# Three input projections by seven half-size products, with compression's input first, and a rearranged routing stretch

## The reference, cut to what matters

```python
proj = rmsnorm(x, g_mix) @ w_in                      # 256 tokens x 1024, w_in 1024 x 4896
q, k_cmp, v_cmp, k_slc, v_slc, k_win, v_win, g_nsa, x_m, o_pre, i_pre, f_pre, gate_a, gate_b = split(proj)
y_a = nsa_mixer(...)       # compress k_cmp/v_cmp (two small layers, gelu), softmax over 15 blocks,
                           # plus 8 heads over all 256 keys
y_b = mlstm_mixer(...)     # conv over x_m, silu, per head recurrence in parallel form, sigmoid(o_pre)
x = x + (sigmoid(gate_a) * (y_a @ w_up_a) + sigmoid(gate_b) * (y_b @ w_up_b)) @ w_o_mix
x = x + cross_attention(rmsnorm(x, g_x), rmsnorm(mem, g_mem))
logits = rmsnorm(x, g_ffn) @ w_router + b_router     # 32 experts, top 4, ties by index
y = sum over the 4 chosen experts of gate * down(swiglu(x @ w_gu[e] + b_gu[e]))
out = rmsnorm(x + y, g_final)
```

## Time and profile before

| | |
|---|---|
| median of three runs | 1264.41 us |
| profiled execution | 1264.81 us |
| its span, first to last instruction | 1263.1 us |
| TensorE busy | 1211.4 us (96%) |
| VectorE busy | 385.0 us (30%) |
| read from HBM | 453.00 MB, 359 GB/s over the span |
| start of the first expert's products | 356.36 us |

### The profile page before, as it was taken

One profiled execution on the slowest core, in us unless ns is written; L12 is line 12 of the kernel. 1 busy time (PEld: TensorE's weight loads), 2 busy tenths in 40 slices (PEclk: granted clock), 3 DMA queues, 4 the chain that ended last, 5 costly groups with the idle time before them and its releaser, 6 DMA issues.

```text
span 1263.1 us, 15787 instructions
## 1 busy us (share of the span) xinstructions
PE 1211.4 (96%) x6541; PEld 604.4 (48%) x6541; DVE 385.0 (30%) x778; ACT 147.5 (12%) x335; POOL 7.9 (1%) x33
## 2 busy tenths in 40 slices
PE   9999999999999999999999999999989999999987
PEld 8879995869443333433333334333333344333322
DVE  3386677483731112211111122111111132111112
ACT  2224333004100000000000000000000000000001
POOL 1000000000000000000000000000000000000000
PEclk9999999999999999999999999999999999999999
DMA  9952323479479999999999999999999999999996
GB/s 334 319 213 75 109 96 146 177 277 357 173 307 423 428 429 427 428 428 428 429 428 430 427 429 430 428 429 427 429 430 428 429 427 428 428 427 428 428 427 266
DMA packets 61319, 454.74 MB, mean 360 GB/s; under 512 B 7325, under 2 KB 14169, under 8 KB 35161
## 3 DMA queue, kind: packets, MB, share of 16 engines
q1 hardware_dynamic: 59032, 452.49, 87.1%
q10 hardware_dynamic: 2240, 1.58, 0.4%
HBM read 453.00 MB, written 1.05 MB: 359 GB/s over the span
## 4 chain that ended last, share of the span: by engine, by line
PE 67%; DMA 30%; DVE 1%; SPq 1%; issue 1%; ACT 0%; DVEq 0%; ACTq 0%
PE ps L1478 30%; DMA r_odd<-in_w_gu_dram 18%; DMA ring<-in_w_down_dram 12%; PE ps L1171 6%; PE ps L987 4%; PE ps L1311 4%; PE ps L1455 3%; PE ps L1471 3%; PE ps L1370 2%; PE ps L1169 2%; PE ps L1555 2%; PE ps L994 2%; PE ps L1040 1%; PE ps L1586 1%; PE ps L1581 1%
## 5 line engine op out<-in xcount | busy, mean ns | idle before, releaser
L1478 PE MATMUL ps<-r_odd,r_memT 128*64 128x512 f32 x1024 | 225.4, 593 | 13.2 <-DMA r_odd<-in_w_gu_dram 13.2
L1478 PE MATMUL ps<-ring,r_memT 128*64 128x512 f32 x1024 | 225.8, 594 | 12.6 <-DMA ring<-in_w_gu_dram 11.9
L2303 DVE TENSOR_SCALAR r_ga<-ps 128x512 f32<-128x512 f32 x32 | 22.1, 691 | 632.8 <-PE ps L1478 632.8
L1478 PE MATMUL ps<-ring,r_ga 128*64 128x512 f32 x760 | 173.2, 604 | 11.4 <-DMA ring<-in_w_down_dram 11.4
L1478 PEld LDWEIGHTS ps<-r_odd,r_memT 128*64 128x64 f32 x1024 | 73.0, 137 | 162.9 <-issue 135.4
L1478 PEld LDWEIGHTS ps<-ring,r_memT 128*64 128x64 f32 x1024 | 71.8, 137 | 160.8 <-issue 136.1
L1478 PEld LDWEIGHTS ps<-ring,r_ga 128*64 128x64 f32 x760 | 54.0, 139 | 127.7 <-issue 106.1
L927 ACT ACTIVATE r_ga<-r_ga 128x512 f32<-128x512 f32 x31 | 19.5, 630 | 510.6 <-PE ps L1471 489.2
L1455 PE MATMUL ps<-r_dm,r_x 128*128 128x128 f32 x512 | 65.7, 282 | 0.0
L1471 PE MATMUL ps<-r_ga,r_dm 64*128 64x512 f32 x256 | 63.6, 615 | 0.7 <-ACT r_ga L934 0.7
L1455 PEld LDWEIGHTS ps<-r_dm,r_x 128*128 128x128 f32 x512 | 62.8, 197 | 1.6 <-DVE r_dm L2233 0.8
(11 more groups left out here) (396 smaller groups left out, 1033.1 us busy)
## 6 DMA issues: line engine op xcount, KB each, us to landing
ring<-in_w_gu_dram SPq DMA_DIRECT2D x60, 2048.0 KB, 27.7
r_odd<-in_w_gu_dram SPq DMA_DIRECT2D x60, 2048.0 KB, 28.4
ring<-in_w_down_dram SPq DMA_DIRECT2D x45, 2048.0 KB, 22.6
...
```

The costliest lines, as they stand in the source:

```text
L1478: last = mm(ps[n * SLOTS:(n + 1) * SLOTS, bk, :], stationary_, moving(n), start=start, stop=stop, skip_group_check=True)
L2303: V.tensor_scalar(gact, ps[:, GBK, :], 7.0, None, ALU.min).then_inc(g_limited, 1)
```

## The change

Up to the routing:

- Pieces and groups are put in another order: `kcvs` is loaded and computed first, then `kwg`, `xm`, `phi`, `q`, `op`.
- `xm`, `q` and `op` are each computed by seven half-size products (order 1, 2, 6, 3, 7, 5, 4) instead of 32 (16 for `op`) direct matmuls. Products 1, 6, 7 and 4 of all three share bank 7. Per projection VectorE makes four sums of weight blocks in place and adds four product results, ScalarE copies four. The sigmoid's tanh of `op` becomes one instruction at the end.
- The convolution's taps, the gate rows and the compression's small operations on VectorE are put between these.
- The banks of the groups behind move with it.

Routing: the first half of the router's product stands inside the last projection's transpositions; three of the four residual matmul pairs go behind block 1's gate and up products; the first bias matmuls stand ahead of the slot numbers; the tie-breaking is shorter by two VectorE instructions; the first gather is split in two banks so that the first expert's first piece can start on half of it; the first expert's down pieces are asked for in halves, as soon as the last projection has used up the slot's first half.

The core of the diff:

```diff
-PIECES = ["q", "kcvs", "kwg", "xm", "phi", "op", "ga0", "ga1", "gb0", "gb1",
+PIECES = ["kcvs", "kwg", "xm", "phi", "q", "op", "ga0", "ga1", "gb0", "gb1",
-LAST_USE = {"q": "q1", "kcvs": "ksvs", "kwg": "nw", "xm": "xm1", "phi": "cmpB", "op": "op1",
+LAST_USE = {"q": "qP4", "kcvs": "ksvs", "kwg": "nw", "xm": "xmP4", "phi": "cmpB", "op": "opP4",
...
-    g = ["gmix", "tm0", "tm1", "tm2", "tm3", "rb", "q0", "q1", "vec", "kcvc", "ksvs", "kwvw", "nw", "xm0", "gn", "if", "xm1",
-         "cmpA", "cmpB", "op0", "cmpT", "op1", "cmp2", "te0", "te1", "te2", "te3", "mt", "csA", "csB"]
+    g = ["gmix", "tm0", "tm1", "tm2", "tm3", "rb", "kcvc", "ksvs", "vec", "kwvw", "nw", "xmP1", "xmP2", "gn", "if"]
+    g += [f"xmP{n}" for n in HALF_ORDER[2:]] + ["cmpA", "cmpB"]
+    g += [f"qP{n}" for n in HALF_ORDER] + ["cmpT"] + [f"opP{n}" for n in HALF_ORDER]
+    g += ["cmp2", "te0", "te1", "te2", "te3", "mt", "csA", "csB"]
...
+        if name in chained:
+            pairs.append((name, BANKS - 1))
+            continue
...
-        n = BANKS - 3 if first <= i < last else BANKS
+        n = BANKS - 3 if first <= i < last else BANKS - 1 if first_chain < i < last_chain else BANKS
+        if name == "roP1":
+            turn += (6 - turn) % n
...
-            for name in ("kcvs", "kwg", "xm"):
+            for name in ("kwg", "xm", "phi"):
...
+            down_slot = [ring[:, eslot[name]].rearrange("p (k n) -> p k n", k=4) for name in ("dn0", "dn1")]
+            filled_of(sp, "roP7")
+            sp.dma_start(down_slot[0][:, 0:2], dn_dram[0, 0][:, 0:2]).then_inc(first_down_loaded[0], 16)
+            sp.wait_ge(sums_ready, 10)
+            sp.dma_start(down_slot[1][:, 0:2], dn_dram[0, 1][:, 0:2]).then_inc(first_down_loaded[1], 16)
             filled_of(sp, "roP5")
+            sp.dma_start(down_slot[0][:, 2:4], dn_dram[0, 0][:, 2:4]).then_inc(loaded[eslot["dn0"]], 16)
             odd_half(1, 1, 0)
-            first_block(range(5, 6))
-            filled_of(sp, "rt")
+            filled_of(sp, "roP4")
+            sp.dma_start(down_slot[1][:, 2:4], dn_dram[0, 1][:, 2:4]).then_inc(loaded[eslot["dn1"]], 16)
+            filled_of(sp, "rw")
             odd_half(1, 1, 1)
...
-            copy("op1", so[:, 1], bank("op1"), ACT.Tanh, scale=0.5)
+            for n in (6, 7, 4):
+                half_out("op", n)
+            drained_of(act, "opP2")
+            drained_of(act, "opP5")
+            drained_of(act, "opP4")
+            nc.scalar.activation(r_so, r_so, ACT.Tanh, scale=0.5).then_inc(so_ready, 1)
...
+            def half_product(w, n):
+                i = HALF_WIDE.index(w)
+                a11, a12, a21, a22 = token_blocks(hT)
+                b11, b12, b21, b22 = half_blocks(w)
+                tokens, weight = {1: (a11, b11), 2: (a12, b21), 3: (sums_h[:, 3], b22), 6: (sums_h[:, 1], b11),
+                                  5: (sums_h[:, 0], b22), 7: (sums_h[:, 2], b12), 4: (a22, b21)}[n]
+                if n == 1:
+                    weights(w)
+                elif n != 2:
+                    pe.wait_ge(token_sums_ready, 1)
+                if n in (7, 6, 4, 5):
+                    pe.wait_ge(half_sums, 4 * i + {7: 1, 6: 2, 4: 3, 5: 4}[n])
+                o = begin(f"{w}P{n}")
+                for c in range(1 if w == "op" else 2):
+                    for k in range(4):
+                        first, final = c == 0 and k == 0 and n not in HELD[1:], k == 3
+                        if w == "op":
+                            last = mm(o[:, 0:T], tokens[:, k], weight[:, k], start=first, stop=final, skip_group_check=True)
+                        else:
+                            last = mm(o[:, c * P:(c + 1) * P], weight[:, k, c * P:(c + 1) * P], tokens[:, k],
+                                      start=first, stop=final, skip_group_check=True)
+                end(f"{w}P{n}", last)
...
-            end("xm1", feature_group("xm1", [stationary(w, 2), stationary(w, 3)], hT))
+            for n in HALF_ORDER[2:]:
+                half_product("xm", n)
...
-            weights("op")
-            w = wslot("op", C, 512)
+            for n in HALF_ORDER:
+                half_product("q", n)
...
-            end("op1", token_part(begin("op1"), w, 512, hT, 1))
+            for n in HALF_ORDER:
+                half_product("op", n)
...
             drained_of(pe, "cmp2")
-            drained_of(pe, "q0")
-            drained_of(pe, "q1")
+            for n in (2, 5, 4):
+                drained_of(pe, f"qP{n}")
...
+                    if t == 0 and between:
+                        between()
...
-            project_and_turn("ro", "ox", oxT, "tf", chunks_of("ox"), 1)
+            def router_rows(part):
+                for k in part:
+                    drained_of(pe, f"tf{k // 2}")
+                    j = 32 * (k % 4)
+                    last = mm(bank("rw")[j:j + 32, 0:T], wr[:, k, :], hT[:, k, :], start=(k < 4), stop=(k >= 4),
...
+            def router_first_rows():
+                begin("rw")
+                pe.wait_ge(wr_loaded, 16)
+                router_rows(range(4))
+            project_and_turn("ro", "ox", oxT, "tf", chunks_of("ox"), 1, router_first_rows)
...
-            residual_start(0, 0)
             residual_start(0, 1)
-            pe.wait_ge(wr_loaded, 16)
-            narrow("rw", lambda k: wr[:, k, :], hT, chunks_of("tf"))
-            residual_start(1, 0)
+            end("rw", router_rows(range(4, 8)))
...
+            biases(range(1))
...
+            biases(range(1, 2))
...
+                        last = mm(ps[:, ZBK if first and c < 2 else buf, c * P:(c + 1) * P],
+                                  x_rows[:, t, 2 * q + c // 2, c % 2], place[:, t], start=(t == 0), stop=(t == 1))
+                    if first and c == 1:
+                        last.then_inc(first_gathered, 1)
...
+                if is_block(i, 1):
+                    residual_start(0, 0)
+                    residual_start(1, 0)
+                    residual_start(1, 1)
...
-            biases(range(1))
-            biases(range(1, 2))
+            gather_half(XBK, 0, True)
...
+            def half_difference_of_right(w):
+                b11, b12, b21, b22 = half_blocks(w)
+                dve.wait_ge(loaded[slot_of[w]], need[w])
+                V.tensor_tensor(b12, b22, b12, ALU.subtract).then_inc(half_sums, 1)
+            def half_sum_over_first(w):
+                b11, b12, b21, b22 = half_blocks(w)
+                dve.wait_ge(half_sums, 4 * HALF_WIDE.index(w) + 1)
+                filled_of(dve, f"{w}P1")
+                V.tensor_tensor(b11, b12, b11, ALU.add).then_inc(half_sums, 1)
+            def half_lower_left(w):
+                b11, b12, b21, b22 = half_blocks(w)
+                filled_of(dve, f"{w}P2")
+                drained_of(dve, f"{w}P1")
+                c11 = half_quarter(w, 0, 0)
+                drain(f"{w}P2", V.tensor_tensor(c11, c11, half_bank(w, 2), ALU.add))
+                dve.wait_ge(half_sums, 4 * HALF_WIDE.index(w) + 2)
+                V.tensor_tensor(b21, b21, b11, ALU.subtract).then_inc(half_sums, 1)
+            def half_lower_right(w):
+                b11, b12, b21, b22 = half_blocks(w)
+                filled_of(dve, f"{w}P3")
+                V.tensor_tensor(b22, b22, b11, ALU.subtract).then_inc(half_sums, 1)
+                drained_of(dve, f"{w}P6")
+                c12 = half_quarter(w, 0, 1)
+                drain(f"{w}P3", V.tensor_tensor(c12, c12, half_bank(w, 3), ALU.add))
+            def half_fifth(w):
+                filled_of(dve, f"{w}P5")
+                drained_of(dve, f"{w}P3")
+                c12, c22 = half_quarter(w, 0, 1), half_quarter(w, 1, 1)
+                V.tensor_tensor(c12, c12, half_bank(w, 5), ALU.add)
+                drained_of(dve, f"{w}P7")
+                drain(f"{w}P5", V.tensor_tensor(c22, c22, half_bank(w, 5), ALU.add))
...
+            half_sum_over_first("xm")
+            half_lower_left("xm")
...
+            half_lower_right("xm")
+            half_difference_of_right("q")
+            half_fifth("xm")
+            for n in (2, 5, 4):
+                drained_of(dve, f"xmP{n}")
...
-            dve.wait_ge(gate_e, 1)
-            link(V.tensor_scalar(gflat, gflat, 0.5, 0.5, ALU.mult, ALU.add))
...
-            V.tensor_tensor(rows[:, 7], rows[:, 4], mrow, ALU.add).then_inc(rows_ready, 1)
-            dve.wait_ge(silu_e, 1)
-            link(V.tensor_scalar(r_xc, r_xc, 0.5, 0.5, ALU.mult, ALU.add))
-            V.tensor_tensor(r_xc, r_xc, r_tmp, ALU.mult).then_inc(xc_ready, 1)
+            half_sum_over_first("q")
+            half_lower_left("q")
...
+            half_lower_right("q")
...
+            half_difference_of_right("op")
+            half_fifth("q")
+            half_sum_over_first("op")
...
+            half_lower_left("op")
+            dve.wait_ge(gate_e, 1)
+            link(V.tensor_scalar(gflat, gflat, 0.5, 0.5, ALU.mult, ALU.add))
...
+            half_lower_right("op")
...
```

(17 more changed lines are left out.)

206 lines of the change are left out of this document (108 added, 98 removed).

## The result

The changed kernel is slower: 1268.11 us median of 12 runs (1266.72 to 1270.02) against 1264.38 (1263.39 to 1267.55, 12 runs), ratio 1.0029 with a 95% interval of 1.0021 to 1.0037. The forecast was 1262.6, range 1258.0 to 1265.8.

What follows compares the result with a forecast made beforehand. Expert blocks run at the speed of their weights (DMA, some 907 us); ahead of them TensorE bounds. Front +2.7, routing -4.8, block 1 +0.3 sum to -1.8 us: 1262.6 us, range 1258.0 to 1265.8.

Steps and rivals of the forecast that it cites:

- Steps 1 and 2: Front: half-size products of q, xm, op save 4.7 us; waits for ScalarE's copy in shared bank 7 cost 0.4.
- Step 3: Front: the compressed scores wait for VectorE's copies out of `cmp2`, +1.9 us.
- Step 4: Front: the first scores wait for VectorE's copy that drains `mt`, behind the compressed scores' softmax, +4.2 us.
- Step 5: Front: lower clock in the compressed scores or scores around the two idle stretches, +0.9 us (0 to 3.6).
- rival C: Front: both gaps let the clock fall to half ahead of work, so slower, 1265.3 to 1266.3 us; chance 0.15.
- Step 7: Routing: earlier top 4, shorter tie-breaking, earlier gather and split gather bring the first expert product forward, -4.8 us (-4.0 to -5.4).
- Step 9: Block 1: three residual pairs delay TensorE and a slot's release by 2.9 us, cost +0.3 us (0 to 2.9).
- Steps 6 and 8: Weights in the front land in time, and the first expert's down pieces in halves too: cost 0 each.

Runs made afterwards that it cites:

- e1: Changed kernel with the VectorE copy that drains `mt` moved ahead of the compressed scores' softmax; 1263.08 us, ratio 0.9988 to the kernel before.
- e7: Kernel before with only the routing part of the change, including down pieces in halves and residual pairs in block 1; 1264.15 us, ratio 1.0001.
- e6: Kernel before with only the front of the change (order of pieces, half-size products, bank places), routing as before; 1269.29 us, ratio 1.0043.
- e8: Changed kernel with two of the three residual pairs moved from block 1 into the routing's waits; 1265.21 us, ratio 1.0003 to the kernel before.
- e5: Changed kernel with matmuls of ones issued into the routing's waits; 1266.30 us, ratio 1.0015 to the kernel before.

## Why the prediction was wrong

- Steps 1 and 2, the products and the shared bank: right, 4.2 won instead of 4.7, 0.46 lost instead of 0.4.
- Step 3, +1.9: the wait is there, 1.5, ended by the row named.
- Step 4, +4.2: there, 4.29. e1 takes it away and wins 5.0.
- Step 5, +0.9, is the term of the front that was too small. The half clock cost 1.5 on the compressed scores, 0.6 on the scores and 0.7 on the products in the profiled execution, 2.8 over the before's; the upper bound I wrote was 3.6. I had taken the low end because the kernel before fell without a gap, and argued that the same loss was only moved. It was lengthened: 13.8 us at half instead of 3.4. That is the mechanism of rival C, given 0.15, but by itself it makes 1264.5 of the forecast. Both ends of this comparison are single executions that differ from others of their front: e7 shows the kernel before's front 1.6 faster, e6 and e8 the changed one's 1.3 to 1.4.
- **Step 7, -4.8, is the step that failed.** It measured -1.7 and lies outside its own bounds (-4.0 to -5.4). I counted the removed residual pairs as pure gain, and the bias pair "where TensorE would wait" as free. The pairs had also kept TensorE busy. Without them it idles 1.48 ahead of `slot`, and slot, bias pair and gather run at half clock. That is 2.3 of the 3.1 missing (e5). The other 0.8 is VectorE: the top 4 starts at 350.63, 3.8 behind the last transposition instead of the 3.45 of the forecast, its chain to 353.02 takes 2.4 instead of 2.1, and small hand-overs follow. The clock was weighed for the front and not for the routing, where the diff made such a gap. The Trainium skill, "TensorE: Matmul & The Clock Gate", section "Why this matters for your kernels", warns of gaps between bursts of matmuls; it speaks of longer ones than these 1.48, so that this gap was enough is what the traces here show and not the page.
- Step 9, +0.3: 1.4 by the spans, 0 to 2.9 allowed. The queue's 14 us between request and landing was read as 5 us of slack. The windows show about 2: the queue runs dry 52 to 52.5 behind the first product, and the old request stood at 50.45.
- Steps 6 and 8: no new wait for a weight in the front or a down piece in the traces; 0.
- The sum, term by term, in the profiled executions: front +2.7 forecast and +5.3 measured, routing -4.8 and -1.7, stream +0.3 and +1.4; -1.8 against +5.1. The changed kernel's median stands only 3.7 above before's; the three other profiles of its front, with shorter products, are one reason.

With what steps 5 and 9 really cost, the forecast would be 1265.6 and still inside the range. Step 7 takes it out: its 3.1 lie beyond its bounds, and no rival speaks of the clock in the routing.
